# A decoder layer whose input rows arrive transposed in three column blocks, with the squares summed by a tree

## The chip, the cores and the metric

One core of a Trainium2 chip runs the whole program. The core has five engines with instruction streams of their own: TensorE (PE; its weight loads are listed as PEld), VectorE (DVE), ScalarE (ACT), GpSimd (POOL), and SyncE (SP), which here issues nearly all DMAs. The metric is the device time of one execution in microseconds, so lower is better.

## The reference, cut to what matters

One layer of a decoder: 1024 prompt rows and 64 sample rows (8 sequences of 8 tokens), width 1024, all in float32.

```
h = x * rsqrt(mean(x*x, -1) + 1e-6) * attn_norm_g
z = h @ w_in                    # u_val, u_gate, q, k, v, qi, ki, wi
u = u_val * sigmoid(u_gate)     # then: causal depthwise conv, width 31, LayerNorm, swish
q, k = rope(rms_norm(q)), rope(rms_norm(k));  qi, ki = rope(qi), rope(ki)
score = sum_h wi * relu(qi . ki);  sel = top_256(score)
attn = softmax(q . k[sel]) @ v[sel]
x = x + concat(conv, attn) @ w_out
h = rms_norm(x);  x = x + (silu(h @ w_gate) * (h @ w_up)) @ w_down
```

The change touches the first line, and with it the start of the second and third. Everything from `qi` on stays as it is.

## The kernel before, in words

Every float32 product is made from three matmuls on split operands: x = hi + lo and w = hi + lo, and hi*hi, hi*lo and lo*hi are added in PSUM (`three`, L845 to L849). For h the two halves are the tiles `hi_t` and `lo_t`, [128, 8, 1088]: 8 blocks of 128 channels down the partitions, 1088 rows of x along the free dimension, so h lies there transposed. Weights come in units of 512 KB (unit 0, the columns of the indexer's key and weights, has 320 KB) into two places `w_raw`. POOL splits each into one of six slots `w_hi` and `w_lo` (`split`, L728 and L730), and must wait until PE has used up the unit that was in the slot (`used`).

**Opening.** x is read in nine tiles of rows: 64 sample rows, then eight times 128 prompt rows (`load_x`, three places `xin`). For each tile ACT squares it and adds up the squares of each row in the same instruction (`square_rows`, L1388). POOL turns the sum into the reciprocal root in two instructions (`row_rs`, L736 and L739). DVE multiplies the tile by that and by the gain row `gbc` (`norm_rows`, L1753), PE turns the tile round in eight 128x128 transposes into PSUM (`transpose_rows`, L859), ACT copies the result as `hi_t` (`take_hi`, L1397) and DVE takes `lo_t` = PSUM - `hi_t` (`take_lo`, L1763). POOL splits unit 0 after the third tile's `row_rs`, unit 1 after the sixth's and the others after the ninth's.

**Projections.** When all nine tiles are through, PE multiplies over three column blocks of 384, 384 and 320 rows of x (`BLOCKS`), 24 matmuls a block: first the index keys (`kiw_mm`, three blocks), then the 512 + 512 channels of the gated unit, for each of four channel tiles `ct` the value blocks and then the gate blocks (`u_mm`, eight units, 24 blocks). ACT takes the sigmoid of each gate block (L1429) and DVE multiplies it with the value block (L1859 to L1864). After the three blocks of a channel tile DVE runs a stretch of the convolution's taps, 1024 wide each (`conv_taps`, L1815 and L1819, with the numbers in `U_TAPS`). DVE also rotates the index keys `kiw` (L1770 to L1773). A PSUM bank is taken again only after DVE or ACT has read it, which `glu_mul` and `glu_sig` count. The index query projection (`project(1, ...)`) follows.

All order is written out by hand with semaphores. Each engine works through its stream strictly in order.

## Time and profile before

| quantity | value |
|---|---|
| device time, median of 3 runs | 1702.61 us (1698.61 to 1703.23) |
| the profiled execution, device time | 1696.86 us |
| its span | 1694.8 us |
| PE busy | 1547.6 us (91%) |
| DVE busy | 901.5 us (53%) |
| ACT busy | 429.3 us (25%) |
| POOL busy | 469.5 us (28%) |
| first projection matmul | 43.36 us from the span's start |

The span runs from the first to the last instruction; the device time has 2.1 us more around it. The shares are averages over stages with different limits: the chain of waits that ended last is put at 69% PE and 17% DVE. For this change the first 160 us count, and there the timeline by engine tells more than the shares. In matmul rows the durations overlap, so the pace is the distance from one start to the next.

### The profile page before, as it was taken

Reading aid. Unit: us, or ns where it says so; the run is one execution under the profiler, and the core shown is the slowest. Engines: PE = TensorE matmul, PEld = TensorE weight load, DVE = VectorE, ACT = ScalarE, POOL = GpSimd, SP = SyncE. Lnnn points to the kernel's source line nnn. Section 1 sums busy time; section 2 is a strip of 40 time slices with the busy share of each in tenths; the row PEclk is TensorE's granted clock in tenths of the full one; section 3 lists DMA queues with packets and bytes.
Section 4 is the critical chain, followed back from the end, with each engine's and each line's share of the span. In section 5 each row is a group of like instructions: output and inputs, shape, how many; then the busy total and the mean of one; then the engine's idle time right before and its main releaser. Section 6 shows DMA issues by size and latency. Waiting matters only on the chain.

```text
span 1694.8 us, 24400 instructions
## 1 busy us (share of the span) xinstructions
PE 1547.6 (91%) x9105; PEld 1419.6 (84%) x9105; DVE 901.5 (53%) x1612; ACT 429.3 (25%) x799; POOL 469.5 (28%) x322
## 2 busy tenths in 40 slices
PE   3999998878976866989999999999999999999999
PEld 3998776626764655879998999999999999999999
DVE  5199979998866888443435414334242332423324
ACT  4100148844335553443222010100101000010000
POOL 4433211040340000011523243332534334343320
PEclk9999999989997897888999999999999999999999
DMA  6212100120044332023211011111111111111102
GB/s 200 81 50 78 55 13 20 28 80 1 25 139 154 110 90 69 26 63 131 76 49 38 26 63 38 50 37 37 50 50 40 47 37 50 35 51 41 46 0 105
DMA packets 66895, 100.70 MB, mean 59 GB/s; under 512 B 12129, under 2 KB 46177, under 8 KB 66687
## 3 DMA queue, kind: packets, MB, share of 16 engines
q1 hardware_dynamic: 61970, 94.84, 17.6%
q10 hardware_dynamic: 4853, 4.93, 0.9%
q8 instruction: 42, 0.69, 0.2%
q14 instruction: 30, 0.25, 0.0%
HBM read 87.08 MB, written 13.02 MB: 59 GB/s over the span
## 4 chain that ended last, share of the span: by engine, by line
PE 69%; DVE 17%; issue 7%; ACT 5%; POOL 1%; DMA 1%; SPq 0%; DVEq 0%; ACTq 0%; POOLq 0%
PE ps L847 20%; PE ps L849 20%; PE ps L848 20%; DVE y_e L1819 2%; DVE mcnt L1962 2%; PE ps L1120 1%; DVE y L1819 1%; DVE sm L2120 1%; PE ps L1108 1%; DVE qi_tok L1908 1%; ACT lo_t L1601 1%; ACT rl L1487 1%; PE ps L1092 1%; PE ps L1247 1%; PE ps L1162 1%
## 5 line engine op out<-in xcount | busy, mean ns | idle before, releaser
L847 PE MATMUL ps<-hi_t,w_hi 128*128 128x384 f32 (+3 forms) x1464 | 479.6, 328 | 4.9 <-issue 2.5
L849 PE MATMUL ps<-hi_t,w_lo 128*128 128x384 f32 (+3 forms) x1464 | 478.7, 327 | 0.0
L848 PE MATMUL ps<-lo_t,w_hi 128*128 128x384 f32 (+3 forms) x1464 | 478.3, 327 | 0.0
L847 PEld LDWEIGHTS ps<-hi_t,w_hi 128*128 128x128 f32 (+1 forms) x1464 | 274.8, 188 | 6.7 <-issue 4.5
L848 PEld LDWEIGHTS ps<-lo_t,w_hi 128*128 128x128 f32 (+1 forms) x1464 | 274.8, 188 | 0.6
L849 PEld LDWEIGHTS ps<-hi_t,w_lo 128*128 128x128 f32 (+1 forms) x1464 | 274.6, 188 | 0.6
L2346 DVE TENSOR_TENSOR x<-x,ps 128x384 f32<-128x384 f32 (+1 forms) x264 | 139.4, 531 | 104.7 <-PE ps L849 104.0
L847 PE MATMUL ps<-f_hi,w_hi 128*128 128x384 f32 (+1 forms) x528 | 175.5, 332 | 2.9 <-DVE x L2346 2.5
L849 PE MATMUL ps<-f_hi,w_lo 128*128 128x384 f32 (+1 forms) x528 | 172.8, 327 | 0.0
L848 PE MATMUL ps<-f_lo,w_hi 128*128 128x384 f32 (+1 forms) x528 | 172.7, 327 | 0.0
L830 POOL CAST w_hi<-w_raw 128x1024 fp32r<-128x1024 f32 x60 | 62.8, 1047 | 333.6 <-PE ps L849 333.6
L1730 ACT ACTIVATE sg<-sg 128x384 f32<-128x384 f32 (+1 forms) x66 | 33.3, 508 | 463.5 <-DVE sg L2322 463.5
L832 POOL TENSOR_TENSOR w_lo<-w_raw,w_hi 128x1024 fp32r<-128x1024 f32 x60 | 147.8, 2463 | 4.8
L2332 DVE TENSOR_TENSOR ff<-ps,sg 128x384 f32<-128x384 f32 (+1 forms) x66 | 35.4, 536 | 208.9 <-PE ps L849 208.0
L2322 DVE TENSOR_TENSOR sg<-ps,rs_all 128x384 f32<-128x384 f32 (+1 forms) x66 | 35.2, 536 | 201.9 <-PE ps L849 200.0
L728 POOL CAST w_hi<-w_raw 128x1024 fp32r<-128x1024 f32 (+1 forms) x39 | 43.5, 1117 | 281.1 <-PE ps L849 200.9
L1819 DVE SCALAR_TENSOR_TENSOR y_e<-u,kf,y_e 128x1024 f32<-128x1024 f32 x77 | 114.8, 1490 | 2.5
L847 PE MATMUL ps<-w_hi,hi_t 128*128 128x512 f32 (+1 forms) x256 | 101.3, 396 | 10.1 <-DVEq L1923 5.3
L847 PEld LDWEIGHTS ps<-f_hi,w_hi 128*128 128x128 f32 x528 | 99.1, 188 | 9.6 <-DVE x L2346 9.2
L812 POOL TENSOR_TENSOR sg<-sg,rs_all 128x384 f32<-128x384 f32 (+1 forms) x66 | 63.8, 969 | 140.9 <-ACT sg L1730 140.9
L730 POOL TENSOR_TENSOR w_lo<-w_raw,w_hi 128x1024 fp32r<-128x1024 f32 (+1 forms) x39 | 100.9, 2587 | 3.1
L849 PE MATMUL ps<-w_hi,lo_t 128*128 128x512 f32 (+1 forms) x256 | 100.7, 393 | 0.0
(290 smaller groups left out, 2341.2 us busy)
## 6 DMA issues: line engine op xcount, KB each, us to landing
w_raw<-in_w_gate SPq DMA_DIRECT2D x22, 512.0 KB, 3.5
w_raw<-in_w_up SPq DMA_DIRECT2D x22, 512.0 KB, 3.5
w_raw<-in_w_down SPq DMA_DIRECT2D x22, 512.0 KB, 3.4
w_raw<-in_w_in SPq DMA_DIRECT2D x16, 512.0 KB, 3.6
kt_b<-in_cache_kt SPq DMA_DIRECT2D x48, 128.0 KB, 2.3
v_b<-in_cache_v SPq DMA_DIRECT2D x48, 128.0 KB, 2.4
x<-in_x_t SPq DMA_DIRECT2D x8, 544.0 KB, 8.1
xin<-in_x_prompt SPq DMA_DIRECT2D x8, 512.0 KB, 4.1
```

The costliest lines, as they stand in the source:

```text
L728: pool.tensor_copy(w_hi[:, n % SLOTS, 0:w], w_raw[:, n % RAW, 0:w]).then_inc(split_hi, 1)
L730: pool.tensor_tensor(w_lo[:, n % SLOTS, 0:w], w_raw[:, n % RAW, 0:w], w_hi[:, n % SLOTS, 0:w].bitcast(F32), ALU.subtract).then_inc(split_l ...
L812: pool.tensor_tensor(sg[:, m % 3, 0:z - a], sg[:, m % 3, 0:z - a], rs_all[:, a:z], ALU.mult).then_inc(sg_ready, 1)
L830: pool.tensor_copy(w_hi[:, slot, :], w_raw[:, raw, :]).then_inc(split_hi, 1)
L832: pool.tensor_tensor(w_lo[:, slot, :], w_raw[:, raw, :], w_hi[:, slot, :].bitcast(F32), ALU.subtract).then_inc(split_lo, 1)
L847: pe.matmul(out, a_hi, b_hi, start=first, stop=False)
L848: pe.matmul(out, a_hi, b_lo, start=False, stop=False)
L849: return pe.matmul(out, a_lo, b_hi, start=False, stop=last)
L1819: dve.scalar_tensor_tensor(yp, up, w, yp, ALU.mult, ALU.add).then_inc(tap_done, 1)
L2322: dve.tensor_tensor(sg[:, m % 3, 0:z - a], ps[:, m % 3, 0:z - a], rs_all[:, a:z], ALU.mult).then_inc(gate_taken, 1)
L2332: dve.tensor_tensor(ff[:, m % 2, 0:z - a], ps[:, 3 + m % 3, 0:z - a], sg[:, m % 3, 0:z - a], ALU.mult).then_inc(f_ready, 1)
L2346: dve.tensor_tensor(x1[:, m, a:z], x1[:, m, a:z], ps[:, 6 + q % 2, 0:z - a], ALU.add).then_inc(y_added, 1)
```

## The change

x is read only in its transposed form `in_x_t`, in three column blocks of 384, 384 and 320 rows of x, with one DMA each, into `xt`, [128, 8, 1088]. For each block ACT squares it in two halves without adding up. DVE adds the 8 channel blocks in a tree (`square_sums`), PE adds over the 128 partitions with three matmuls one column wide (`rows_sums`), and DVE scales the mean (`row_means`). POOL takes the power of three columns at once and writes three 128x128 diagonals (`row_rs`), PE multiplies these by a tile of ones, which spreads each row's factor over all partitions (`spread_scales`), and DVE multiplies `xt` by the gain, which is now one number per partition, and by the PSUM result (`norm_tiles`). `take_hi` and `take_lo` now read `xt` in SBUF, in quarters of two channel blocks. The transposes and the gain row are gone. PE starts on the key block of column block 0 as its quarters come, and mixes key blocks and gated blocks of the first channel tile. Value and gate blocks now alternate.

```diff
-        xin = at("xin", 0, [P, 3, D])
-        xn = at("xn", 12288, [P, 2, D])
-        sq = at("sq", 20480, [P, D])
-        gbc = at("gbc", 24576, [P, D])
+        xt = at("xt", 0, [P, KT, ROWS])
+        sq = [[at("sq0", 34816, [P, KT // 2, 384]), at("sq1h", 55296, [P, KT // 2, 384])],
+              [at("sq0_b", 40960, [P, KT // 2, 384]), at("sq1h_b", 64512, [P, KT // 2, 384])]]
+        diag = at("diag", 61440, [P, 3, P])
...
-        kiw_t = at("kiw_t", 20480, [KIW, ROWS])
+        kiw_t = at("kiw_t", 50944, [KIW, ROWS])
...
-        sig = at("sig", 20512, [P, 2, 384])
+        sig = at("sig", 64000, [P, 2, 384])
...
-            return (s + 2) % 8
+            return (3, 5, 6, 4, 7, 2, 0, 1)[s % 8]
+        def halves(j):
+            return [(slice(4 * h, 4 * h + 4), slice(*BLOCKS[j])) for h in range(2)]
+        def quarters(j):
+            return [(slice(2 * q, 2 * q + 2), slice(*BLOCKS[j])) for q in range(4)]
...
-            def load_x(o):
-                t = ALL[o]
-                if o >= 3:
-                    sp.wait_ge(xn_ready, o - 2)
-                src = A["x_sample"] if t == SAMPLE else A["x_prompt"][cols_of(t), :]
-                sp.dma_start(xin[0:rows_of(t), o % 3, :], src).then_inc(x_in[o % 3], 16)
+            def load_x(j):
+                a, z = BLOCKS[j]
+                sp.dma_start(xt[:, :, a:z], A["x_t"].rearrange("(k p) r -> p k r", p=P)[:, :, a:z]).then_inc(x_in[j], 16)
             load_x(0)
-            sp.dma_start(gbc[:, :], A["attn_norm_g"].broadcast_to([P, D])).then_inc(g_in, 16)
-            load_x(1)
-            load_x(2)
             sp.dma_start(kf[:, :], A["kf"]).then_inc(consts_in, 16)
             sp.dma_start(pages[:, :], A["page_table"]).then_inc(consts_in, 16)
             sp.dma_start(kb[:, :], A["kb"]).then_inc(consts_in, 16)
             load_unit(0)
+            load_x(1)
             load_unit(1)
-            for o in range(3, NT):
-                load_x(o)
+            load_x(2)
...
-                    return u_mm, 3 * (n - N_U + 1)
+                    return u_mm, (n - N_U) // 2 * 6 + 5 + (n - N_U) % 2
...
+            def row_rs(j):
+                pool.wait_ge(ms_ready, j + 1)
+                c = slice(3 * j, 3 * j + 3)
+                pool.tensor_tensor(rs[:, c], rs[:, c], half_neg[:, 0:3], ALU.pow).then_inc(rs_ready, 1)
+                pool.wait_ge(rs_ready, j + 1)
+                if j > 0:
+                    pool.wait_ge(rsbc_mm, j)
+                pool.tensor_tensor(diag[:, :, :], ident.unsqueeze(1).broadcast_to([P, 3, P]),
+                                   rs[:, c].unsqueeze(2).broadcast_to([P, 3, P]), ALU.mult).then_inc(diag_ready, 1)
...
-            for o in range(NT):
-                row_rs(o, rows_of(ALL[o]), D)
-                if o in (2, 5):
-                    split(o // 3)
-            for n in range(2, 17):
+            pool.wait_ge(consts_in, 16 * 3)
+            split(0)
+            row_rs(0)
+            row_rs(1)
+            split(1)
+            split(2)
+            row_rs(2)
+            for n in range(NB, 17):
                 split(n)
...
+            def rows_sums(j):
+                pe.wait_ge(sq_summed, j + 1)
+                for t in range(3 * j, 3 * j + 3):
+                    r = rows_of(t)
+                    mm = pe.matmul(ps[0:r, 4, t:t + 1], sq[j % 2][0][:, 0, t % 3 * P:t % 3 * P + r], ones[:, 0:1],
+                                   start=True, stop=True)
+                mm.then_inc(sums_mm, 1)
+            def spread_scales(j):
+                pe.wait_ge(diag_ready, j + 1)
+                for t in range(3 * j, 3 * j + 3):
+                    r = rows_of(t)
+                    mm = pe.matmul(ps[:, 5 + j, t % 3 * P:t % 3 * P + r], ones[0:r, :], diag[0:r, t % 3, 0:r],
+                                   start=True, stop=True)
+                mm.then_inc(rsbc_mm, 1)
...
+            def key_block(j):
+                a, z = BLOCKS[j]
+                if j == 0:
+                    pe.wait_ge(split_lo, N_KIW + 1)
                 for k in range(KT):
+                    if k % 2 == 0:
+                        pe.wait_ge(lo_ready, 4 * j + k // 2 + 1)
                     mm = three(ps[0:KIW, j, 0:z - a], *unit(N_KIW, k, KIW), hi_t[:, k, a:z], lo_t[:, k, a:z],
                                k == 0, k == KT - 1)
                 mm.then_inc(kiw_mm, 1)
+            def gated_block(s):
+                ct, j, g = s // 6, s % 6 // 2, s % 2
+                n = N_U + 2 * ct + g
+                a, z = BLOCKS[j]
+                if j == 0:
+                    pe.wait_ge(split_lo, n + 1)
+                if s == 6:
+                    pe.wait_ge(kiw_evac, 1)
+                if s >= 8:
+                    before = s - 8
+                    pe.wait_ge(glu_sig if before % 2 else glu_mul, 3 * (before // 6) + before % 6 // 2 + 1)
+                for k in range(KT):
+                    mm = three(ps[:, u_bank(s), 0:z - a], *unit(n, k, P), hi_t[:, k, a:z], lo_t[:, k, a:z],
+                               k == 0, k == KT - 1)
+                mm.then_inc(u_mm, 1)
+            pe.wait_ge(consts_made, 1)
+            pe.wait_ge(pool_step, 1)
+            rows_sums(0)
+            rows_sums(1)
+            spread_scales(0)
+            spread_scales(1)
+            key_block(0)
+            gated_block(0)
+            rows_sums(2)
+            gated_block(1)
+            spread_scales(2)
+            key_block(1)
+            gated_block(2)
+            gated_block(3)
+            key_block(2)
+            gated_block(4)
...
+            for s in range(5, 6 * CT):
+                gated_block(s)
...
+            def square_rows(j):
+                act.wait_ge(x_in[j], 16)
+                if j > 1:
+                    act.wait_ge(sums_mm, j - 1)
+                for h, (ks, rows) in enumerate(halves(j)):
+                    act.activation(sq[j % 2][h][:, :, 0:rows.stop - rows.start], xt[:, ks, rows], ACT.Square
+                                   ).then_inc(sq_ready, 1)
+            def take_hi(j):
+                for q, (ks, rows) in enumerate(quarters(j)):
+                    act.wait_ge(xn_ready, 4 * j + q + 1)
+                    act.activation(hi_t[:, ks, rows], xt[:, ks, rows], ACT.Copy).then_inc(hi_ready, 1)
...
+            square_rows(0)
+            square_rows(1)
+            take_hi(0)
+            square_rows(2)
+            take_hi(1)
+            take_keys(0)
+            take_hi(2)
+            take_gate(0)
+            take_keys(1)
+            take_gate(1)
+            take_keys(2)
...
+            take_gate(2)
...
+            def square_sums(j):
+                n = BLOCKS[j][1] - BLOCKS[j][0]
+                first, second = sq[j % 2]
+                for h, part in enumerate((first, second)):
+                    dve.wait_ge(sq_ready, 2 * j + h + 1)
+                    ins = dve.tensor_tensor(part[:, 0:2, 0:n], part[:, 0:2, 0:n], part[:, 2:4, 0:n], ALU.add)
+                link(ins)
+                link(dve.tensor_tensor(first[:, 0:2, 0:n], first[:, 0:2, 0:n], second[:, 0:2, 0:n], ALU.add))
+                dve.tensor_tensor(first[:, 0, 0:n], first[:, 0, 0:n], first[:, 1, 0:n], ALU.add).then_inc(sq_summed, 1)
+            def row_means(j):
+                dve.wait_ge(sums_mm, j + 1)
+                if j == 2:
+                    dve.tensor_scalar(rs[0:SR, SAMPLE:NT], ps[0:SR, 4, SAMPLE:NT], 1.0 / (C * D), RMS_EPS / (C * C),
+                                      ALU.mult, ALU.add)
+                c = slice(3 * j, min(3 * j + 3, SAMPLE))
+                dve.tensor_scalar(rs[:, c], ps[:, 4, c], 1.0 / (C * D), RMS_EPS / (C * C), ALU.mult, ALU.add
+                                  ).then_inc(ms_ready, 1)
+            def norm_tiles(j, first, last):
+                a, z = BLOCKS[j]
+                dve.wait_ge(rsbc_mm, j + 1)
+                for k in range(first, last):
+                    ins = dve.scalar_tensor_tensor(xt[:, k, a:z], xt[:, k, a:z], kf[:, K_GA + k:K_GA + k + 1],
+                                                   ps[:, 5 + j, 0:z - a], ALU.mult, ALU.mult)
+                    if k % 2 == 1:
+                        ins.then_inc(xn_ready, 1)
+            def take_lo(j, q):
+                ks, rows = quarters(j)[q]
+                dve.wait_ge(hi_ready, 4 * j + q + 1)
+                dve.tensor_tensor(lo_t[:, ks, rows], xt[:, ks, rows], hi_t[:, ks, rows].bitcast(F32), ALU.subtract
+                                  ).then_inc(lo_ready, 1)
...
+            square_sums(0)
+            row_means(0)
+            square_sums(1)
+            row_means(1)
+            for j in range(NB):
+                norm_tiles(j, 0, 4)
+                if j == 1:
+                    square_sums(2)
+                take_lo(j, 0)
+                norm_tiles(j, 4, 6)
+                if j == 1:
+                    row_means(2)
+                take_lo(j, 1)
+                norm_tiles(j, 6, 8)
+                take_lo(j, 2)
+                take_lo(j, 3)
+            dve.wait_ge(lo_ready, 4 * NB)
...
+            gate_values(0)
+            gate_values(1)
...
-        "x_prompt": a["x_prompt"][0], "x_sample": a["x_sample"].reshape(SR, D),
```

What is left out are the new semaphores, the gain's place `K_GA` among the constants `kf`, constants that count `rs_ready`, `lo_ready` and `x_in` further on, and the move of the gate code into functions (`take_gate` on ACT, `gate_values` on DVE) with the same instructions.

PE's stream at its start, before: 72 transposes and then the key blocks.

```order
L838 UNCONDITIONAL_BRANCH
L859 MATMUL ps<-kf,xn 128x64 x8
L859 MATMUL ps<-kf,xn 128x128 x64
L847 MATMUL ps<-hi_t,w_hi 80x384
L848 MATMUL ps<-lo_t,w_hi 80x384
L849 MATMUL ps<-hi_t,w_lo 80x384
```

The same place now, with the semaphores that each row waits for.

```order
L926 MATMUL ps<-ones,sq_50 128x1 [waits sq_summed,pool_step,consts_made]
L926 MATMUL ps<-ones,sq_50 128x1 x2
L926 MATMUL ps<-ones,sq_b 128x1 [waits sq_summed]
L926 MATMUL ps<-ones,sq_b 128x1 x2
L935 MATMUL ps<-diag,ones 128x128 [waits diag_ready]
L935 MATMUL ps<-diag,ones 128x128 x2
L935 MATMUL ps<-diag,ones 128x128 [waits diag_ready]
L935 MATMUL ps<-diag,ones 128x128 x2
L858 MATMUL ps<-hi_t,w_hi 80x384 [waits lo_ready,split_lo]
```

The sums of block 1 stand ahead of the spreading for block 0, and both spreadings stand ahead of the first key block.

POOL's stream in the opening, before, from its sixth row's power on (`rs` is the reciprocal root, `w_hi` and `w_lo` the split of a weight unit).

```order
L736 TENSOR_SCALAR rs<-ms 128x1
L739 TENSOR_TENSOR rs<-rs,half_neg 128x1
L728 CAST w_hi<-w_raw 128x1024
L730 TENSOR_TENSOR w_lo<-w_raw,w_hi 128x1024
L736 TENSOR_SCALAR rs<-ms 128x1
```

POOL's stream now, from its first split on.

```order
L734 CAST w_hi<-w_raw 128x640 [waits raw_in0,consts_in]
L736 ISA
L736 TENSOR_TENSOR w_lo<-w_raw,w_hi 128x640 [waits split_hi]
L743 TENSOR_TENSOR rs<-rs,half_neg 128x3 [waits ms_ready]
L747 TENSOR_TENSOR diag<-kf,rs 128x384 [waits rs_ready]
L743 TENSOR_TENSOR rs<-rs,half_neg 128x3 [waits ms_ready]
L747 TENSOR_TENSOR diag<-kf,rs 128x384 [waits rsbc_mm,rs_ready]
L734 CAST w_hi<-w_raw 128x1024 [waits raw_in1]
L736 TENSOR_TENSOR w_lo<-w_raw,w_hi 128x1024 [waits split_hi]
L734 CAST w_hi<-w_raw 128x1024 [waits raw_in0]
L736 TENSOR_TENSOR w_lo<-w_raw,w_hi 128x1024 [waits split_hi]
L743 TENSOR_TENSOR rs<-rs,half_neg 128x3 [waits ms_ready]
```

The nine small powers have become three of three columns, each with a diagonal behind it. Unit 0 is split ahead of the first power, units 1 and 2 between the second and the third.

DVE's stream now, from the end of block 1's sums to the first two quarters of block 0.

```order
L1799 TENSOR_TENSOR sq_b<-sq_b 128x384 [waits dve_step]
L1808 TENSOR_SCALAR rs<-ps 128x3 [waits sums_mm]
L1816 SCALAR_TENSOR_TENSOR xt<-xt,kf,ps 128x384 [waits rsbc_mm]
L1816 SCALAR_TENSOR_TENSOR xt<-xt,kf,ps 128x384 x3
L1825 TENSOR_TENSOR lo_t<-xt,hi_t 128x2x384 [waits hi_ready]
L1816 SCALAR_TENSOR_TENSOR xt<-xt,kf,ps 128x384 [waits rsbc_mm]
L1816 SCALAR_TENSOR_TENSOR xt<-xt,kf,ps 128x384
L1825 TENSOR_TENSOR lo_t<-xt,hi_t 128x2x384 [waits hi_ready]
```

The norm of block 0 stands behind all work on the sums of block 1, and `lo_t` is now taken from two SBUF operands.

## Rows read from the trace of the kernel before

**Rows 1.** The chain of waits, in order of time (start, length, what).

```profile
3.81 7.02 DMA kb<-in_kb
43.36 0.58 PE ps L847
107.17 3.37 DVE y_e L1819
```

**Rows 2.** The timeline by engine, opening and first splits (start, us, engine, line, what).

```profile
4.67 1.06 ACT L1388 ACTIVATE sq<-xin 64x1024 f32<-64x1024 f32 x1 [2.64 <-DMA xin<-in_x_sample]
25.07 1.04 POOL L728 CAST w_hi<-w_raw 128x1024 fp32r<-128x1024 f32 x1
25.16 2.03 DVE L1753 SCALAR_TENSOR_TENSOR xn<-xin,rs,gbc 128x1024 f32<-128x1024 f32 x1 [0.66 <-POOL rs L739]
26.19 3.21 POOL L730 TENSOR_TENSOR w_lo<-w_raw,w_hi 128x1024 fp32r<-128x1024 f32 x1
27.11 1.28 DVE L1763 TENSOR_TENSOR lo_t<-ps,hi_t 128x512 fp32r<-128x512 f32 x2
...
58.22 2.40 POOL L730 TENSOR_TENSOR w_lo<-w_raw,w_hi 128x1024 fp32r<-128x1024 f32 x1
```

**Rows 3.** The timeline, key and first gated blocks: PE's pace, ACT's reads.

```profile
44.38 0.53 PE L847 MATMUL ps<-hi_t,w_hi 128*80 128x384 f32 x1
44.70 0.53 PE L848 MATMUL ps<-lo_t,w_hi 128*80 128x384 f32 x1
...
49.37 0.49 ACT L1413 ACTIVATE kiw_t<-ps 80x384 f32<-80x384 f32 x1 [7.43 <-PE ps L849]
53.48 0.49 ACT L1413 ACTIVATE kiw_t<-ps 80x384 f32<-80x384 f32 x1 [3.63 <-PE ps L849]
...
82.11 0.44 ACT L1429 ACTIVATE sig<-ps 128x320 f32<-128x320 f32 x1 [3.02 <-PE ps L849]
```

**Rows 4.** Stretches: length, busy PE, PEld, DVE, ACT, POOL, clock, DMA share, GB/s.

```profile
4.00:6.00 2.00, 0.00 (x0) 0.00 (x0) 0.00 (x0) 1.15 (x2) 0.09 (x1) 1.00 0.96 303
8.00:10.00 2.00, 0.00 (x0) 0.00 (x0) 0.33 (x2) 0.86 (x2) 0.76 (x2) 1.00 1.03 381
...
1687.00:1688.00 1.00, 1.00 (x9) 1.00 (x8) 0.49 (x1) 0.00 (x0) 0.00 (x0) 1.00 1.03 372
```

**Rows 5.** Groups by shape: count, busy us, mean ns, idle before.

```profile
L1632 ACT ACTIVATE ysq<-y 128x1536 f32<-128x1536 f32 x2 | 2.9, 1468 | 0.0
L2346 DVE TENSOR_TENSOR x<-x,ps 128x384 f32<-128x384 f32 x176 | 96.4, 552 | 70.5 <-PE ps L849 69.7
L1910 DVE TENSOR_TENSOR acc<-acc,qi_tok 128x1024 f32<-128x1024 f32 x1 | 1.2, 1226 | 0.0
L795 POOL TENSOR_TENSOR lnr<-lnr,half_neg 128x3 f32<-128x3 f32 x3 | 2.6, 859 | 246.2 <-DVE lnr L2170 246.2
L812 POOL TENSOR_TENSOR sg<-sg,rs_all 128x384 f32<-128x384 f32 x44 | 44.6, 1015 | 91.1 <-ACT sg L1730 91.1
L1326 PE MATMUL ps<-diag,ones 128*128 128x128 f32 x16 | 2.5, 287 | 1.5 <-DVE diag L2312 1.5
```

**Rows 6.** The timeline, where the index keys are rotated and the taps begin.

```profile
59.34 1.42 DVE L1770 TENSOR_TENSOR rt<-kiw,kf 128x128 f32<-128x128 f32 x1 [16.08 <-ACT kiw L1417]
...
62.09 0.17 DVE L1801 TENSOR_SCALAR wi_tok<-kiw 64x16 f32<-64x16 f32 x1
...
70.34 1.04 POOL L728 CAST w_hi<-w_raw 128x1024 fp32r<-128x1024 f32 x1 [9.72 <-PE ps L849]
...
82.58 0.43 DVE L1862 TENSOR_TENSOR u<-ps,sig 128x256 f32<-128x256 f32 x1 [2.90 <-ACT sig L1429]
```

**Rows 7.** PE's waits between 110 and 210 us (us in total, times, longest).

```profile
PE ps L847 <- DVE u L1859: 1.6, 1, 1.6
```

**Rows 8.** Two later stretches, with columns as in Rows 4.

```profile
85.00:107.00 22.00, 22.00 (x136) 22.00 (x135) 20.99 (x19) 1.43 (x3) 6.07 (x4) 1.00 0.17 48
...
236.00:800.00 564.00, 456.08 (x2669) 359.32 (x2669) 420.32 (x853) 287.81 (x528) 78.47 (x52) 0.89 0.22 68
```

173 lines of the change are left out of this document (49 added, 124 removed).

## The prediction, made before the changed kernel was run

> **What bounds the kernel now.** I read the chain of waits first. In the first 107 us it is made of the opening (the first matmul of a projection comes at 43.36), then of PE, and from 107 us on of DVE's taps [rows 1]. The stretches of time confirm it: between 85 and 107 us PE is busy in 22.00 of 22.00 us and DVE in 20.99 [rows 8], and in the whole stretch from 110 to 210 us PE waits once, 1.6 us, for a DVE product [rows 7]. So both engines are nearly full there, side by side, and both start from the end of the first channel tile, at about 82.0 us (ACT reads its last gate block at 82.11) [rows 3]. What the opening gives back is kept only if both move: PE by its own start, DVE by the moment at which it can begin the taps (82.58 before [rows 6]). Everything behind is issued by counts of finished work and not at a fixed time, so I carry the shift on to the end one to one.
>
> The opening is a chain through four engines and nine tiles. The timeline shows POOL's splits in it twice: a DVE instruction that meets one takes 2.03 us [rows 2], and PE gets its next tile later.
>
> **When x is there.** The first load before, 0.26 MB, landed at 4.67 [rows 2], and `kb`, with 2.54 MB issued up to it (x 0.26 and two of 0.52, gain 0.52, `kf` 0.53, `kb` 0.18), at 3.81 + 7.02 = 10.83 [rows 1]. That is landing = 3.97 us + bytes / 370 GB/s. The new runs of 1536 bytes are no worse: the result's store, with the same runs, goes at 372 GB/s, and the opening's stretches show 303 to 381 [rows 4]. So block 0 (128 x 8 x 384 x 4 = 1.57 MB) lands at 8.2, the constants (2.29 MB) at 10.2, unit 0 (2.61 MB) at 11.0, block 1 (4.19 MB) at 15.3, block 2 (6.02 MB) at 20.2. At 303 GB/s block 1 would come 2.5 us later.
>
> **Squares and factors.** ACT squares 128x1536 in 1.47 [rows 5], so block 1's halves are ready at 16.8 and 18.3. The tree's wide adds, 768 elements, cost 0.92 (three quarters of the 1.226 for 1024), the last about 0.5 [rows 5]. Block 0's tree is done well before. For block 1: 18.3 + 0.92 + 0.92 + 0.5 + 0.3 of hops = 20.9. POOL's `row_rs(0)` (0.86 for the power, 1.0 for the diagonals by the multiply of 128x384 [rows 5]) lies beside it, and one add runs into it: I add 0.8, bounds 0 and 1.0, and have 21.7. PE's three sums and then three spreadings of block 0, at 0.29 each [rows 5], end at 23.5. This place decides the opening: PE's in-order stream has `rows_sums(1)` ahead of `spread_scales(0)`, and DVE `square_sums(1)` ahead of the norm, so block 0 waits for block 1's load though its own diagonals are ready by about 19.
>
> **Block 0 on DVE and the port.** Eight norms with a PSUM operand at 0.55 and four `take_lo` of 768 elements at 0.92 [rows 5] are 8.1 us. Added to them comes a collision that the change makes. Before, a DVE instruction with two SBUF operands (`xn`, issued at 25.16) took until 27.19, which is 1.08 behind the end of POOL's cast (25.07 + 1.04), and then POOL's `w_lo`, issued at 26.19, took 3.21, where one that came first (58.22) took 2.40. `take_lo`, which read PSUM and SBUF, ran at 0.64 each beside the same `w_lo` [rows 2]. Now `take_lo` reads two SBUF tiles, and so do the tree's adds. POOL splits units 1 and 2 from about 25.0 (`row_rs(1)` runs 23.1 to 25.0) to 32 or later, right across block 0. Nothing in the trace has this pairing in this place. Lower bound: no collision, 0. Upper bound: the first two `take_lo` each wait nearly a whole `w_lo`, 2 x 2.3 = 4.6. Laid out instruction by instruction, the first waits 0.6 for the cast, the second about 1.2, and the last 0 or 2.2; I take 2.6. `lo_t` of block 0 is then complete at 23.5 + 8.1 + 2.6 = 34.2.
>
> The Trainium skill states this as a rule (SBUF — State Buffer, section Who interferes with whom): a VectorE instruction with two SBUF inputs and a GpSimd instruction that reads SBUF block each other wholly, and whichever issues first holds the port. The rows above agree with it, 1.08 us behind the cast's end. By it the collision cannot be nothing; a reader who trusted only the unhindered durations would put the gain 2.6 us higher.
>
> **PE.** The key block of block 0 follows quarter by quarter. Its last six matmuls, at the pace of 0.32 that PE had in its first 3 us before (44.38 to 44.70 [rows 3]), end at 36.1. Before, this block was read by ACT at 49.37 [rows 3]: 13.3 us later. From there the same blocks follow, at 4.11 us for 384 columns (49.37 to 53.48 [rows 3]). Differences: + 3 sums and 3 spreadings for block 2 at 0.29, 1.7 us; + 0.5 for more matmuls at the slow pace, since PE has gaps in block 0 (bounds 0 and 1.7, a whole further stretch); + 0.3 for hops; - 0.5, because the key copies now lie beside gated blocks. 13.3 - 1.7 - 0.5 - 0.3 + 0.5 = 11.3. PE reaches the end of the first channel tile at about 70.7.
>
> Is anything else late on the way? Block 1 on DVE: 34.2 + 8.1 + the tree of block 2 (3 x 0.8 + 0.4) and about 2 of waits = 47 to 50. PE starts that key block at 36.1 + 4.6 + 0.9 + 4.1 + 0.9 = 46.6 and needs its last quarter at 49.7, so it is just met. Block 2 on DVE ends near 60, PE wants it at 59 and its last quarter at 61.6. The factor of block 2: DVE gives the mean at about 42, POOL's 0.86 + 1.0 end by 44.3, PE asks at 45.7. Splits 3 to 5 wait behind that on POOL until 44.3 and end at 55; PE wants unit 3 at 70.7. ACT's table load of 1.3 us for the sigmoid now stands inside this stretch, where ACT has room.
>
> **DVE's start of the taps.** Unit 1 used to be done a whole unit ahead of unit 2, and POOL's split into its slot ran at 70.34 to 73.9, with DVE idle [rows 6]. Now units 1 and 2 are used up 3.5 us apart. POOL's next split falls on the rotation of the index keys, whose first instruction took 1.42 before and ended 0.14 behind a `w_lo` that ran from 58.22 to 60.62 [rows 2, 6]. The rotation must be through before DVE takes the last gated product (it stands ahead in DVE's stream). The key transposes end 3.5 us before the tile's end and ACT's copies 1.3 later, so it starts at -2.2 us, is held to -0.8 by `w_lo`, has 0.3 and then 1.5 of instructions left (60.76 to 62.26 before [rows 6]), and meets the next cast for another 1.04: it ends 2.1 after the tile's end, where the last product used to start 0.5 after it. So DVE moves by 11.3 - 1.6 = 9.7 us. Bounds: 0 and 2.8 in place of 1.6. Since PE waits for DVE at the third tile's end [rows 7], DVE's shift is the one kept.
>
> **Sum.** 1694.8 - 9.7 = 1685.1 of span, plus the 2.1 around it, 1687.2 of device time for a profiled execution. The profiled execution before (1696.86) lies 5.75 below the median 1702.61, so on the median's scale I say 1693.
>
> **Rivals.**
> A, no collision: POOL and DVE interleave without loss in block 0 and at the rotation. Gain 9.7 + 2.6 + 1.6 = 13.9, 1688.7. For it: 0.64 us of `take_lo` beside a split. Against it: that one read PSUM.
> B, the taps lose: POOL's splits for a pair of units now come back to back, six pairs' halves fall into the taps up to 155 us, and each may cost DVE some 0.8 more. Gain 9.7 - 5 = 4.7, 1698. Against it: in number the splits stay the same and each held DVE before too.
> C, slower: the clock. Between 236 and 800 us the granted clock is 0.89 with PE busy in 456.1 us [rows 8], and 1.00 between 85 and 107, so it varies in the part that I only shift. If a shifted start met a mean grant lower by 0.02, that would cost 456 x 0.02 / 0.89 = 10 us and eat all; from 0.03 on (15 us, 1708) the kernel is slower by 0.3%. For it only that the grant is not a function of the code. Against it: three runs before lay within 4.6 us.
> D, the change doesn't do what it says: block 1 comes at 303 GB/s, 2.5 us later, and the collisions take their upper bounds (2.0 and 1.2 more). Gain 4.0, 1698.6.
>
> **How the numbers follow.** Forecast (gain 7.5 to 12) 0.55, A 0.17, B 0.13, D 0.10, C 0.05. About 0.3%, 5 us, is what a measurement of this kernel can tell from no change, so faster means below 1697.5. Forecast and A are faster, 0.72, and of B and D, which lie at that edge, nearly half, 0.10: 0.82. Same 0.13, slower 0.05. The range 1686.5 to 1699 reaches past A by 2 us for a quicker load or tree, and takes in B and D.
>
> **What would show it.** The first key matmul at about 27 and the last of block 0 at 36; `row_means(1)` at 22 to 23; `take_lo` instructions of 1.5 to 3 us in block 0 beside 0.92 for undisturbed ones; ACT's third sigmoid read, the tile's end, at 71, the first tap near 73.5; PE's wait in the place of group 7 longer than 1.6 us. If x's block 1 lands after 18, the load was mis-sized. If the taps start 9.7 earlier and the total is not, the loss lies in the taps or later, and the stretches from 73 to 150 and from 236 to 800 us tell which.

## The result, and the profile after

| | before | changed |
|---|---|---|
| median device time | 1702.61 us (1698.61 to 1709.15, 5 runs) | 1688.20 us (1687.31 to 1693.12, 5 runs) |
| span of the profiled execution | 1694.8 us | 1686.4 us |
| PE busy | 1547.6 us | 1545.0 us |
| DVE busy | 901.5 us | 917.8 us |
| POOL busy | 469.5 us | 475.3 us |

The ratio is 0.9925, with a 95% interval of 0.9900 to 0.9951. That is faster by 12.8 us (8 to 17). The two profiled executions lie 8.4 us apart, as the one before was 5.75 below its median. The time lies in the predicted range, 4.8 us below the predicted value. PE has 2.6 us less to do, and DVE and POOL have more, so the gain does not come from less work. What moved is when PE starts.

The opening of the changed kernel, from the timeline by engine (start, length, engine, line, operation; in brackets the idle time before it and what ended it).

```profile
7.70 1.48 ACT L1425 ACTIVATE sq<-xt 128x1536 f32<-128x1536 f32 x1 [5.67 <-DMA xt<-in_x_t]
14.93 1.48 ACT L1425 ACTIVATE sq_b<-xt 128x1536 f32<-128x1536 f32 x1 [4.37 <-DMA xt<-in_x_t]
20.92 1.44 PE L926 MATMUL ps<-ones,sq_b 128*128 128x1 f32 x6 [4.63 <-DVE sq_b L1799]
22.39 0.16 DVE L1808 TENSOR_SCALAR rs<-ps 128x3 f32<-128x3 f32 x1 [1.53 <-PE ps L926]
23.89 2.19 DVE L1816 SCALAR_TENSOR_TENSOR xt<-xt,kf,ps 128x384 f32<-128x384 f32 x4 [1.33 <-PE ps L935]
25.89 2.34 POOL L736 TENSOR_TENSOR w_lo<-w_raw,w_hi 128x1024 fp32r<-128x1024 f32 x1
25.99 3.05 DVE L1825 TENSOR_TENSOR lo_t<-xt,hi_t 128x768 fp32r<-128x768 f32 x1
29.19 0.58 PE L858 MATMUL ps<-hi_t,w_hi 128*80 128x384 f32 x1 [2.66 <-DVE lo_t L1825]
30.02 0.94 DVE L1825 TENSOR_TENSOR lo_t<-xt,hi_t 128x768 fp32r<-128x768 f32 x1
31.93 2.96 DVE L1825 TENSOR_TENSOR lo_t<-xt,hi_t 128x768 fp32r<-128x768 f32 x2
34.08 0.61 PE L858 MATMUL ps<-hi_t,w_hi 128*80 128x384 f32 x1 [0.79 <-DVE lo_t L1825]
37.69 0.52 PE L860 MATMUL ps<-hi_t,w_lo 128*80 128x384 f32 x1
38.01 0.40 PE L858 MATMUL ps<-hi_t,w_hi 128*128 128x384 f32 x1
```

ACT reads x at 7.70 and 14.93, so the load went as the 370 GB/s said (8.2 and 15.3). The norm begins at 23.89, behind the sums of block 1. The first `take_lo` took 3.05 us and ended after the `w_lo` that began 0.10 before it. An undisturbed one took 0.94. Block 0's `lo_t` is complete at 34.9. The last matmul of the key block starts at 37.69, and the next block at 38.01. Only behind that do starts lie 0.17 to 0.18 apart and no longer 0.32.

The rows that answer to [rows 3] and [rows 6]: the third gate block's sigmoid, the rotation of the index keys and the first taps of the changed kernel, from the same view.

```profile
69.41 2.24 DVE L1830 TENSOR_TENSOR rt<-kiw,kf 128x128 f32<-128x128 f32 x1 [7.49 <-ACT kiw L1464]
72.06 0.44 ACT L1448 ACTIVATE sig<-ps 128x320 f32<-128x320 f32 x1 [2.69 <-PE ps L860]
73.28 2.43 POOL L736 TENSOR_TENSOR w_lo<-w_raw,w_hi 128x1024 fp32r<-128x1024 f32 x1
73.36 2.37 DVE L1832 TENSOR_TENSOR rt<-kiw,kf 64x8 f32<-64x8 f32 x1
76.05 0.41 DVE L1877 TENSOR_TENSOR u<-ps,sig 128x256 f32<-128x256 f32 x1
76.82 0.81 DVE L1905 TENSOR_SCALAR y_e<-u,kf 128x1024 f32<-128x1024 f32 x1
77.66 15.81 DVE L1909 SCALAR_TENSOR_TENSOR y_e<-u,kf,y_e 128x1024 f32<-128x1024 f32 x12
...
143.32 0.44 ACT L1448 ACTIVATE sig<-ps 128x320 f32<-128x320 f32 x1 [6.71 <-DVE u L1874]
```

The same taps before, DVE's timeline.

```profile
83.36 2.91 DVE L1815 TENSOR_SCALAR y_e<-u,kf 128x1024 f32<-128x1024 f32 x1
86.31 18.50 DVE L1819 SCALAR_TENSOR_TENSOR y_e<-u,kf,y_e 128x1024 f32<-128x1024 f32 x12
```

An instruction on 64x8 numbers took 2.37 us, for as long as POOL's `w_lo` ran. It took 0.15 where no split lay beside it. The first tap came 6.5 us earlier, and not 9.7. But the 13 taps then took 16.65 us (77.66 + 15.81 - 76.82) in place of 21.45: the two splits in question had met the rotation, and until 92.34 POOL did nothing beside the taps.

PE's waits of the changed kernel between 110 and 210 us, to be read beside [rows 7], and between 26 and 110 us (total, times, longest).

```profile
PE ps L858 <- DVE u L1874: 0.2, 1, 0.2
...
PE ps L858 <- DVE lo_t L1825: 3.5, 2, 2.7
```

The wait of 1.6 us became 0.2. The shift can be followed: 10.05 us at the third sigmoid (82.11 to 72.06), 11.6 at the last gate sigmoid (154.89 to 143.32), which is 10.05 and, but for 0.1, the 1.4 of that wait. It is 11.9 at 227 us and 11.9 at 444 (POOL's first power of `hk`, 456.36 before and 444.45 now), 9.7 at a split of weights at 783 (792.43 to 782.77) and 8.4 at the end.

Stretches of the two kernels, before and then changed, with columns as in [rows 4].

```profile
456.00:800.00 344.00, 271.31 (x1885) 232.21 (x1884) 214.10 (x428) 153.02 (x312) 37.71 (x31) 0.86 0.29 93
800.00:1680.00 880.00, 872.75 (x5267) 864.34 (x5266) 304.36 (x542) 98.16 (x190) 314.32 (x210) 1.00 0.13 44
```

```profile
456.00:800.00 344.00, 271.75 (x1890) 235.93 (x1889) 212.71 (x427) 155.40 (x314) 35.00 (x32) 0.83 0.30 96
800.00:1680.00 880.00, 873.35 (x5263) 865.27 (x5263) 304.72 (x545) 95.59 (x188) 310.14 (x208) 1.00 0.13 44
```

From 456 to 800 us the granted clock is 0.86 before and 0.83 now. From 800 us on it is 1.00 in both. The profiled execution before was a quick one of its kernel: from the power of `hk` at 456.36 to its end it took 1238.4 us, while the changed kernel and the ten variants below, with the same work there, took 1241.9 to 1247.1. So I do not lay these 3 us at the change's door. The medians, which differ by more than the profiled pair, do not show them.

### The profile page after: what moved, and what is told of

The parts are those of the page before. It is cut to its first block, busy times and chain, and to the rows that moved or that the text cites. A ratio compares the mean times of both kernels' runs of the same rounds, so it can differ in the third digit from the quotient of the medians.

```text
span 1686.4 us, 24298 instructions
## 1 busy us (share of the span) xinstructions
PE 1545.0 (92%) x9069; PEld 1419.3 (84%) x9069; DVE 917.8 (54%) x1638; ACT 427.7 (25%) x781; POOL 475.3 (28%) x310
## 4 chain that ended last, share of the span: by engine, by line
PE 71%; DVE 17%; issue 6%; ACT 5%; DMA 1%; SPq 0%; POOL 0%; DVEq 0%; ACTq 0%
PE ps L858 21%; PE ps L860 20%; PE ps L859 20%; DVE y_e L1909 2%; DVE mcnt L2041 2%; PE ps L1154 1%; DVE y L1909 1%; PE ps L1142 1%; DVE sm L2199 1%; ACT rl L1528 1%; ACT lo_t L1642 1%; PE ps L1126 1%; DMA xt<-in_x_t 1%; PE ps L1196 1%; PE ps L1127 1%
## 5 line engine op out<-in xcount | busy, mean ns | idle before, releaser
L858 PE MATMUL ps<-hi_t,w_hi 128*128 128x384 f32 (+2 forms) x1464 | 481.5, 329 | 5.8 <-DVE lo_t L1825 3.5
L860 PE MATMUL ps<-hi_t,w_lo 128*128 128x384 f32 (+2 forms) x1464 | 480.2, 328 | 0.0
L859 PE MATMUL ps<-lo_t,w_hi 128*128 128x384 f32 (+2 forms) x1464 | 479.9, 328 | 0.0
L734 POOL CAST w_hi<-w_raw 128x1024 fp32r<-128x1024 f32 (+1 forms) x39 | 48.2, 1236 | 264.7 <-PE ps L860 179.6
```

The costliest lines, as they stand in the source:

```text
L734: pool.tensor_copy(w_hi[:, n % SLOTS, 0:w], w_raw[:, n % RAW, 0:w]).then_inc(split_hi, 1)
L858: pe.matmul(out, a_hi, b_hi, start=first, stop=False)
L859: pe.matmul(out, a_hi, b_lo, start=False, stop=False)
L860: return pe.matmul(out, a_lo, b_hi, start=False, stop=last)
```

## Experiments

Each ratio is to the kernel before, run beside it on the same chip. Its median moved between 1700.8 and 1702.6 us, so ratios compare between sections and times less well. "Third sigmoid" is ACT's read of the third gate block, 72.06 in the changed kernel. "Last sigmoid" is the last one of the gated unit, 143.32. Both come from the one profiled execution of each kernel. The ratio is clear to 0.1 to 0.25%, 1.6 to 4 us.

The third sigmoid is not the same in every execution of the same code. The run with the rotation ahead of the splits (below) changes nothing ahead of POOL's split at 67.97 us. Its PE rows in the opening, and its third sigmoid:

```profile
29.05 0.58 PE L860 MATMUL ps<-hi_t,w_hi 128*80 128x384 f32 x1 [2.66 <-DVE lo_t L1827]
31.66 0.51 PE L862 MATMUL ps<-hi_t,w_lo 128*80 128x384 f32 x1
31.98 0.36 PE L860 MATMUL ps<-hi_t,w_hi 128*80 128x384 f32 x1
36.10 0.33 PE L860 MATMUL ps<-hi_t,w_hi 128*128 128x384 f32 x1
70.07 0.44 ACT L1450 ACTIVATE sig<-ps 128x320 f32<-128x320 f32 x1 [2.69 <-PE ps L862]
```

The first key matmul comes behind the same wait of 2.66 us as in the changed kernel. But the pace rises with the tenth matmul, at 31.98, the next block starts at 36.10 and not at 38.01, and the third sigmoid comes 2.0 us earlier. Two more runs have the same code up to the end of the first key block. In the one with the late start the pace rose with the twelfth matmul, 3.6 us behind the first. In the one with the key blocks one behind the other all 24 ran at 0.32. So the profiled execution of the changed kernel drew a long slow stretch, and an edit's effect on the third sigmoid has to be read against 70.07, the execution with the early rise, wherever the pace rose early too. The distance from the third sigmoid to the last is steadier: 71.2 to 71.5 us where PE waited 0.3 or less for a gated product between 110 and 210 us, and 73.7 to 73.9 where it waited 2.6 to 2.8.

| kernel | first key matmul | pace rises | third sigmoid | last sigmoid | power of `hk` | ratio |
|---|---|---|---|---|---|---|
| changed | 29.19 | 38.0 | 72.06 | 143.32 | 444.45 | 0.9925 |
| rotation ahead of the splits | 29.05 | 32.0 | 70.07 | 144.01 | 448.40 | 0.9947 |
| idle multiplications | 29.82 | 30.5 | 70.01 | 141.45 | 443.33 | 0.9928 |
| split in the gap | 29.61 | 33.8 | 69.78 | 141.04 | 443.93 | 0.9922 |
| both of these | 29.80 | at once | 69.69 | 143.37 | 445.27 | 0.9950 |
| all three edits | 30.48 | 31.2 | 69.54 | 143.47 | 450.69 | 0.9952 |
| block 0 first | 26.68 | 30.7 | 70.79 | 142.07 | 443.62 | 0.9922 |
| block 0 first, idle multiplications | 30.42 | at once | 70.98 | 142.43 | 443.39 | 0.9958 |

### No overlap: where does the gain come from?

```diff
+            rows_sums(2)
+            spread_scales(2)
+            pe.wait_ge(lo_ready, 4 * NB)
             key_block(0)
             gated_block(0)
-            rows_sums(2)
             gated_block(1)
-            spread_scales(2)
```

(`take_hi(2)` of ACT stands ahead of `take_keys(0)`, which would otherwise block it.)

> The changed kernel, but PE starts its first key block only when h of all three column blocks is split (it does the third block's sums and spreading before that; ACT takes the third block's hi ahead of the first key copy). Theory 1, that the gain comes from PE starting on block 0 while DVE still works on blocks 1 and 2: the new opening is by itself longer than the old one (the last take_lo ends at 57.4 us in the changed kernel, about 55 here, against 43.3 before), so the third sigmoid read comes at about 92 instead of 72.1 (82.1 before) and the time is 1705 to 1713, slower than before. Theory 2, that one load per block, the tree and the missing transposes make the opening itself shorter: all of h is ready by 43 or earlier and the time stays below 1700.

Measured: 1711.68 us, ratio 1.0049 (1.0033 to 1.0064). PE's waits between 26 and 110 us in this kernel:

```profile
PE ps L926 <- DVE sq L1800: 13.3, 1, 13.3
PE ps L858 <- DVE lo_t L1826: 9.7, 1, 9.7
PE ps L935 <- POOL diag L747: 3.2, 1, 3.2
```

The third sigmoid came at 94.61, the last at 168.28. Without the overlap the new opening is slower than the old one by 0.5%, 8.3 us (5.6 to 10.9). The whole gain, and more, is that PE multiplies block 0 while blocks 1 and 2 are being prepared.

### The key blocks one behind the other

```diff
             key_block(0)
-            gated_block(0)
             rows_sums(2)
-            gated_block(1)
             spread_scales(2)
             key_block(1)
-            gated_block(2)
-            gated_block(3)
             key_block(2)
-            gated_block(4)
+            for s in range(5):
+                gated_block(s)
```

(ACT takes the key copies and the gates in the same new order.)

> The changed kernel with PE's three key blocks one behind the other and the gated blocks after them (ACT's copies in the same order), all else the same: PE still starts on block 0 while DVE works on. Theory 1, that the mixing of gated blocks between the key blocks is what keeps PE busy while DVE works on blocks 1 and 2: PE waits near 17 us in all, key block 2 ends at about 58, the third sigmoid read comes at 82 to 83, the gain of the opening is gone and the time is 1698 to 1702. Theory 2, that starting early on the keys is enough: the third sigmoid read comes before 76 and the time stays below 1693.

Measured: 1700.60 us, ratio 1.0000 (0.9987 to 1.0013). The third sigmoid came at 81.34, against 82.11 in the kernel before. PE's waits from 26 to 110 us:

```profile
PE ps L858 <- DVE lo_t L1822: 5.1, 4, 2.7
PE ps L935 <- POOL diag L747: 3.7, 1, 3.7
PE ps L926 <- DVE sq L1796: 1.7, 1, 1.7
```

PE waited 10.5 us in all, where 17 had been expected, and ACT read the last key block at 57.0, where 58 had been expected. So the order of PE's blocks decides. x in column blocks and the tree bring nothing unless gated blocks lie between the key blocks: three key blocks of 4.1 us use up h faster than DVE makes it, which ends `lo_t` of the three blocks at 34.9, 48.2 and 57.4 in the changed kernel. Value and gate blocks alternate here too, so that part of the change brings nothing by itself either.

### A late start: does a shift at 70 us reach the end?

```diff
+            for i in range(3):
+                sp.dma_start(late_k[0][:, 0, :], A["w_gate"][0:P, :]).then_inc(x_in[2], 16)
+                sp.wait_ge(x_in[2], 16 * (i + 1))
             load_x(0)
```

(ACT's wait for block 2 counts these three loads too.)

> The changed kernel, with three loads of 0.5 MB one after the other, each awaited, ahead of the first load of x; nothing reads them. It delays the whole opening by about 11 us and changes nothing else. Theory 1, that a shift of the opening passes to the end one to one: the third sigmoid read comes at about 83 and the time is 1698 to 1700, the gain of the change gone. Theory 2, that the later part gives back or takes most of a shift (clock or DVE): the time moves by less than 6 us from the changed kernel's.

Measured: 1700.11 us over 12 runs, ratio 0.9982 (0.9972 to 0.9991). The third sigmoid moved by 8.4, the same sigmoid row reads:

```profile
80.46 0.44 ACT L1451 ACTIVATE sig<-ps 128x320 f32<-128x320 f32 x1 [2.69 <-PE ps L863]
```

The last sigmoid moved by 8.4 too (151.72), the values' copies at 393 us by 8.4 (401.0), and the time by 0.57%, some 9.7 us; with both intervals that is 5 to 14. ACT's first read of x came 10.2 later (17.89), close to the 11 expected. The other 1.8 us are PE's pace, which rose here with the twelfth matmul: from ACT's first read of x to the third sigmoid it is 62.6 us here, 62.5 in the run with the rotation ahead of the splits, and 64.4 in the changed kernel. The question is answered all the same: a shift of the opening is kept, one to one as far as the ratio can tell. The run without the overlap allows less: 12.5 us at the third sigmoid, 12.2 at the power of `hk`, and 5.6 to 10.9 in the total.

### Block 0 first: the wait for block 1 by program order

```diff
             rows_sums(0)
-            rows_sums(1)
             spread_scales(0)
-            spread_scales(1)
+            rows_sums(1)
             key_block(0)
+            spread_scales(1)
             gated_block(0)
```

(On DVE, likewise, `square_sums(j + 1)` now stands behind the first norms of block j.)

> The changed kernel with block 0's spreading on PE and its first norms on DVE ahead of block 1's squares tree. Theory 1, that block 0 waits for block 1's load by program order: the first norm starts at about 20.4 instead of 23.9, DVE loses its idle stretches of 1.5 and 1.3 us, block 0's last take_lo ends near 32.5 instead of 34.9 and the third sigmoid read comes 1.5 to 2.5 us before 72.1. Theory 2, that DVE has the same work to do up to there and is full: the first norm is earlier, the last take_lo of block 0 is not, and the third sigmoid read stays within 0.5 us of 72.1. The total moves by 0 to 2.5 us, too little for its interval; the trace decides.

Measured: 1688.73 us, ratio 0.9922 (0.9909 to 0.9935). DVE's rows:

```profile
19.82 2.19 DVE L1816 SCALAR_TENSOR_TENSOR xt<-xt,kf,ps 128x384 f32<-128x384 f32 x4 [3.58 <-PE ps L935]
29.15 3.18 DVE L1825 TENSOR_TENSOR lo_t<-xt,hi_t 128x768 fp32r<-128x768 f32 x2
34.37 2.19 DVE L1816 SCALAR_TENSOR_TENSOR xt<-xt,kf,ps 128x384 f32<-128x384 f32 x4 [2.04 <-PE ps L935]
```

The norm starts 4.1 us earlier and `lo_t` of block 0 is complete 2.6 earlier (32.3). Against that stand a new wait of 2.04 us of DVE for the factors of block 1, and one of 1.8 of PE for the sums of block 2. The third sigmoid (70.79) comes 1.3 before the changed kernel's, but PE's pace rose early here, and against the 70.07 of the same opening with an early rise it comes 0.7 late. The pair with idle multiplications says the same: 70.98 with block 0 first, 70.01 without. That block 0 waits for block 1 is real, but neither pair shows time lost by it at the third sigmoid.

### POOL's split moved into its gap: the collision

```diff
             row_rs(0)
-            row_rs(1)
             split(1)
+            row_rs(1)
             split(2)
```

(SP, besides, waits for block 1's sums behind its load of unit 3, before it loads the samples' state and the further units.)

> The changed kernel with POOL's split of unit 1 moved ahead of the second row_rs, into POOL's idle time from 19.5 to 22.6 us (the loads of the conv state wait for the second sums). Theory 1, that POOL's split holds block 0's take_lo: the first take_lo takes about 1.0 instead of 3.05 us and block 0's last take_lo ends 1.5 to 2 us before 34.9. Theory 2, that the collision only moves: the split now meets the tree's adds of block 1, the first norm starts 1 to 2 us after 23.9, and block 0's last take_lo ends within 0.5 us of 34.9.

Measured: 1689.93 us, ratio 0.9922 (0.9905 to 0.9940). DVE's `take_lo` of block 0 and two of PE's rows:

```profile
26.41 3.05 DVE L1826 TENSOR_TENSOR lo_t<-xt,hi_t 128x768 fp32r<-128x768 f32 x1
32.36 1.95 DVE L1826 TENSOR_TENSOR lo_t<-xt,hi_t 128x768 fp32r<-128x768 f32 x2
...
33.51 0.52 PE L859 MATMUL ps<-hi_t,w_hi 128*80 128x384 f32 x1
34.26 0.33 PE L859 MATMUL ps<-hi_t,w_hi 128*80 128x384 f32 x1
```

One collision (2.1) stayed, because split 2 took the place of split 1. The other (1.0) went. DVE was 0.6 us earlier on block 0 (34.3), but the third sigmoid came 2.3 us earlier (69.78). The difference is in PE's rows. Here PE did not have to wait at 34 (0.8 us saved), and its pace rose from 0.32 to 0.17 at 33.8 and not at 38.0: the last ten matmuls or so of the block took 0.15 less each, 1.5 us. That was in neither theory. It is not the edit's doing either, since the pace also rose early without it: against 70.07 only 0.3 us are left. Between the two runs with idle multiplications (70.01 and 69.69) it is 0.3 as well.

### Idle multiplications ahead of the first key block

To test whether PE's pace in the first key block hangs on its idle time, nine multiplications (18 matmul rows) of 128 columns fill PE's wait for the first quarter. Their result is not used.

```diff
             spread_scales(1)
+            for i in range(9):
+                pe.matmul(ps[:, 3, 0:P], ones[:, :], ident, start=True, stop=True)
             key_block(0)
```

> The changed kernel with nine more matmuls of 128x128 float32 on PE between the second spreading (ends at 26.5 us) and the first key block (29.2 us), where PE is idle; nothing reads their result. Theory 1, that PE runs block 0's key block at half pace (0.32 us from start to start, all 24 in the changed kernel) because it was idle before: with PE kept busy the pace of 0.17 comes by the end of the first six, the block ends at about 36.0 instead of 38.0, held by DVE's last quarter, and the third sigmoid read comes at about 70.1 instead of 72.1. Theory 2, that the end of the block is set by DVE's quarters anyway: it ends at 37.5 or later and the third sigmoid read is within 0.5 us of 72.1.

Measured: ratio 0.9928 (0.9906 to 0.9949), 1690.08 us; one execution of six, at 8358.7 us, was an outlier and has no part in the ratio. PE's rows:

```profile
26.12 4.05 PE L975 MATMUL ps<-kf,ones 128*128 128x128 f32 x18
29.82 0.65 PE L858 MATMUL ps<-hi_t,w_hi 128*80 128x384 f32 x1
30.49 0.33 PE L860 MATMUL ps<-hi_t,w_lo 128*80 128x384 f32 x1
30.66 0.34 PE L858 MATMUL ps<-hi_t,w_hi 128*80 128x384 f32 x1
```

The key block begins 0.6 us later than in the changed kernel and the next block starts 2 us sooner (36.04 against 38.01), and the third sigmoid comes 2.05 earlier (70.01). These are theory 1's numbers. But the run with the rotation ahead of the splits has them without the idle multiplications: 36.10 and 70.07. So the edit is shown to change the pace, quick from the first, second or third matmul on in all four runs that have it, while in all eight traces without it the pace stayed low for 2.9 us or longer from the first key matmul on. It is not shown to save time: where the pace rises by itself before 34, DVE's last quarter sets the end of the block in either case. Nor does the total show anything: 1.9 us (141.45 at the last sigmoid) is below what the ratio tells.

### The rotation ahead of the splits

```diff
                     pool.wait_ge(*used(n - SLOTS))
+                if n == SLOTS + 1:
+                    pool.wait_ge(kiw_ready, 1)
                 pool.tensor_copy(w_hi[:, n % SLOTS, 0:w]
```

> The changed kernel, with POOL's split into the slot of unit 1 (the one at 67.97 us in the changed kernel) held until DVE has rotated the index keys. Theory 1, that POOL's splits hold the rotation and so the taps: the rotation's first instruction takes about 0.3 instead of 2.24 us and the first tap starts 3 to 4 us ahead of 76.8; the two splits then fall on the taps, so the last sigmoid read stays within 0.5 us of 143.3 and the time with it, since PE waits only 0.2 us there. Theory 2, that the late taps cost time: the last sigmoid read and the total come 2 us or more earlier.

Measured: 1693.13 us, ratio 0.9947 (0.9929 to 0.9964). The rotation's first instruction took 0.29 us and not 2.24:

```profile
67.42 0.29 DVE L1832 TENSOR_TENSOR rt<-kiw,kf 128x128 f32<-128x128 f32 x1 [7.49 <-ACT kiw L1466]
...
PE ps L860 <- DVE u L1876: 2.8, 1, 2.8
```

The first tap came at 72.94, 3.9 earlier; 2.0 of that are the early rise of PE's pace, so the edit gave 1.9. But the 12 taps behind it took 18.49 us and not 15.81, PE waited 2.8 for DVE's product, and the last sigmoid came 0.7 later (144.01). Counted from the third sigmoid, it came 73.9 behind and not 71.3, so the edit lost 2.7. A split held off the rotation costs the taps as much, or more. Theory 1 held in that the gain at the first tap is gone at the last sigmoid, but the taps lost more than it said, and the early opening hid most of that loss.

### Three edits at once, then without the rotation's

The first has the three edits above, the second the split in the gap and the idle multiplications alone.

> Three edits to the changed kernel at once: the split of unit 1 ahead of the second row_rs, the nine idle-time matmuls ahead of the first key block, and the split into unit 1's slot held until the keys are rotated. Theory 1, that they add up where they act: block 0's key block ends near 35.5, the third sigmoid read comes at 69 to 70, the first tap at 70.5 to 71.5, and the last sigmoid read 2 to 3 us ahead of 143.3; the time is 1685 to 1688. Theory 2, that DVE's taps set the third tile's end once the opening is shorter: PE waits there for 1.5 us or more, and the last sigmoid read gains less than 1.5 us.

> The changed kernel with two edits at once: POOL splits unit 1 ahead of the second block's power, and PE has nine idle multiplications of 128 columns ahead of the first key block. The third edit of the run of three, the rotation ahead of the splits, is left out. Theory 1 (the start of the tile's end pays, and the rotation's edit was what lost it again): the first key block ends near 35.5, ACT's third sigmoid read comes at 69.3 to 70.1, the last gate sigmoid before 155 us at 140.5 to 141.5, PE waits less than 0.6 us for a gated product between 110 and 210 us, and the time is 1 to 3 us below that of the changed kernel beside the same kernel before, a ratio of 0.990 to 0.992. Theory 2 (both edits give the same 2 us, the earlier rise of PE's pace, and DVE sets the rest): third read 70 to 70.5, last sigmoid 141.5 or later, ratio 0.992 to 0.993. Either way the gain over the changed kernel is near or below what the measurement tells.

Measured: 1693.64 us, ratio 0.9952 (0.9935 to 0.9969), and 1692.54 us, ratio 0.9950 (0.9935 to 0.9966). The third sigmoid came at 69.54 and 69.69, the earliest of all, the last at 143.47 and 143.37, no earlier than in the changed kernel. For the first that is theory 2 (PE waits 2.8 in the place in question). In the second I had expected 140.5 to 141.5, and for both a better ratio than the changed kernel's. The taps show why. First the changed kernel, then the run of two edits: POOL's cast for the last channel tile and DVE's nine taps ahead of the third tile's last products.

```profile
130.25 12.51 DVE L1909 SCALAR_TENSOR_TENSOR y_e<-u,kf,y_e 128x1024 f32<-128x1024 f32 x9
139.74 1.95 POOL L734 CAST w_hi<-w_raw 128x1024 fp32r<-128x1024 f32 x1 [13.96 <-PE ps L860]
```

```profile
128.08 14.73 DVE L1912 SCALAR_TENSOR_TENSOR y_e<-u,kf,y_e 128x1024 f32<-128x1024 f32 x9
137.37 1.04 POOL L735 CAST w_hi<-w_raw 128x1024 fp32r<-128x1024 f32 x1 [13.78 <-PE ps L861]
...
PE ps L859 <- DVE u L1877: 2.6, 1, 2.6
```

In the one the cast waited for a tap (1.95 us) and the taps ran on. In the other the cast took 1.04, as long as an undisturbed one, and the nine taps took 2.2 us more. Which engine comes first is decided by a few tenths of a microsecond: the cast began 67.7 us behind the third sigmoid in both, and the nine taps 58.2 behind it in the one and 58.4 in the other. PE then waits 2.6, and the 2.4 us of a better opening are gone. With this wait of 2.6 to 2.8 the runs have 0.9947, 0.9950 and 0.9952; with one of at most 0.3 the changed kernel and three others have 0.9922 to 0.9928. The groups are some 4 us apart, but the intervals of most pairs still overlap, and the run below (wait 0.3, ratio 0.9958) stands with the wrong group. At the power of `hk`, 300 us further on, the three with the long wait are 0.8 (two edits), 4.0 (rotation alone) and 6.2 us (three edits) behind the changed kernel, and the three without it 0.5 to 1.1 ahead. So for the total I take this as likely, and as shown only in the traces up to there.

### Block 0 first, with the idle multiplications

> The changed kernel with block 0's factors and norm put ahead of block 1's sums on PE and DVE, and PE's nine idle multiplications of 128 columns ahead of the first key block. Theory 1 (two gains that add up, each read alone: 1.3 us of the third sigmoid read from the order, 2.0 from the pace): third read at 69.0 to 69.6, last gate sigmoid near 140.5, ratio about 0.990. Theory 2 (the order's run had the quick pace early in the first key block already, from its fifth matmul's place on, so the idle multiplications only delay the first key matmul): third read 70.3 to 71.0, last sigmoid 141.5 to 142.5, ratio 0.992 as with the order alone.

Measured: 1693.43 us, ratio 0.9958 (0.9942 to 0.9974). The third sigmoid came at 70.98, the last at 142.4, PE waited 0.3: theory 2, since PE's pace rose at 30.7 with block 0 first alone, and the idle multiplications only put the first key matmul off (30.42 against 26.68). The opening is 0.9 us ahead of the changed kernel's, and 1.0 behind that of the idle multiplications alone, and yet the ratio is worse than that of either edit alone. The traces do not show why; its profiled span was 1687.3 where the median would have some 1691.5, and at the power of `hk` it was still 1.1 ahead of the changed kernel. That stays open, and neither theory's ratio for it was met. No version here beats the changed kernel by what can be measured.

## Why the prediction was right, and where not

**The load, 370 GB/s.** Right to 0.5 us on both blocks.

**The tree and the factor, norm at 23.5.** It was 23.89. Right, with its reason: block 0 waits for block 1. The prediction called this the place that decides the opening. It is not, as far as two pairs of traces tell: with block 0 first the norm came 4.1 us earlier, and the third sigmoid no earlier than in a trace with an early rise of PE's pace and without that edit.

**The collision in block 0, 2.6 us.** `lo_t` complete at 34.2 predicted, 34.9 measured. The norm was 0.4 late, and the collisions cost 2.1 in the first quarter (3.05 - 0.94) and 1.0 in the last two (2.96, against 1.95 in the run with the split in the gap), 3.1 in place of 2.6. Rival A (none) is out. But I had spread them over the quarters, and the first one alone cost 2.1, which is why the first key matmul came at 29.19 and not at 27. `w_lo` had begun at 25.89, 0.10 ahead of it, and ended at 28.23; the `take_lo` ended 0.81 behind that. The Trainium skill's rule (SBUF — State Buffer, section Who interferes with whom), that the one which issues first holds the port, agrees with it.

**The slow pace, +0.5 (bounds 0 and 1.7).** This term is not a constant of the code. In the profiled execution of the changed kernel all 24 matmuls of the key block ran at 0.32, and the block ended at 38.0 and not at 36.1, where I had let it end with the last quarter of `lo_t`: 1.9 us, just beyond my upper bound. In the run with the rotation ahead of the splits, with the same opening, the pace rose with the tenth matmul and the block ended at 36.1, as predicted. The waits of 2.66 us ahead of the first matmul are the same in both, so they do not decide it, and what does stays open. At the third sigmoid I had said about 71; the two executions have 72.06 and 70.07.

**DVE's start of the taps, +1.6, and PE's wait longer than 1.6.** The mechanism was right, its size too low and its consequence wrong. The rotation met both splits, 2.24 and 2.37, and the first tap came at 76.82 and not 73.5: DVE's start moved by 6.5 us where PE's moved by 10.05, which is 3.5 in place of 1.6. But a collision does not multiply: the splits which met the rotation were missing in the taps, which got back 4.8 us, and PE's wait fell to 0.2. The step "DVE's shift is the one kept" fails. PE's is: 10.05, and 1.4 of wait on top. The run with the rotation ahead of the splits shows the trade from the other side.

**The shift is kept to the end.** Right: 11.6 us at 143 us, 11.9 at 444, and about one to one in the run with the late start, though the run without the overlap kept less (12.2 at 444, 5.6 to 10.9 in the total), and why stays open. In the profiled pair the span's gain (8.4) is below these by what follows 444 us, where the execution before was a quick one. So the predicted 9.7 was too small by about 2: PE's 11.3 became 10.05 in this execution (12.0 by the third sigmoid of the one with the early rise), and what I took off for DVE (1.6) became a gain of 1.4. That the errors are of opposite sign is luck.

**The scale of the median.** Predicted 1687.2 for a profiled execution, measured 1688.2. But that is also the changed kernel's median, while the one before lay 5.75 below its own. The ratio, over all runs, says 12.8 us, near the 11.9 read at 444 us; the prediction of 1693 is 4.8 above the median by those 2 us and by this scatter of single executions.

**The rivals.** A was nearest in time (1688.7) for another reason: not because nothing collides, but because collisions only move. B is excluded for this kernel (PE's wait is 0.2) and seen in others: in the runs with a wait of 2.6 to 2.8 the taps lose what the opening gave. C did not show beyond 3 us. D is out, since the load was on time.
